# Waiting for both projection banks before the gate product of a feed-forward round

## The reference

```python
def swiglu(h, w13, w2):
    g, u = jnp.split(h @ w13, 2, axis=-1)
    return (jax.nn.silu(g) * u) @ w2
...
        x = x + swiglu(rmsnorm(x, norm_ffn_g[i]), f_w13[i], f_w2[i])
```

## Time and profile before

| | |
|---|---|
| median of 3 runs | 2007.06 us (2005.67 to 2007.57) |
| profiled execution, its own time | 2005.67 us |
| its span, first to last instruction | 2003.9 us |
| PE busy | 1915.3 us, 96% of the span |
| DVE busy | 1376.5 us, 69% |
| ACT busy | 923.3 us, 46% |
| mean granted clock of TensorE | 0.986 of full speed |

### The profile page before, as it was taken

One profiled execution on the slowest core, in us unless ns is written; L12 is line 12 of the kernel. 1 busy time (PEld: TensorE's weight loads), 2 busy tenths in 40 slices (PEclk: granted clock), 3 DMA queues, 4 the chain that ended last, 5 costly groups with the idle time before them and its releaser, 6 DMA issues.

```text
span 2003.9 us, 32582 instructions
## 1 busy us (share of the span) xinstructions
PE 1915.3 (96%) x13424; PEld 1741.9 (87%) x13424; DVE 1376.5 (69%) x1577; ACT 923.3 (46%) x990; POOL 46.3 (2%) x65
## 2 busy tenths in 40 slices
PE   6999988999999988999999999999998999999999
PEld 6998887777777778999989999996878999999998
DVE  4777975766677656766667646668997666676565
ACT  4544843655666554443345444334334333444332
POOL 0000000000000000001101000000000000000000
PEclk8999999999999999999999999999999999999999
DMA  7553352787677756555554376553313655555553
GB/s 217 183 168 99 112 160 78 283 294 268 251 286 282 289 164 181 190 184 194 189 168 135 105 215 203 196 173 126 106 64 130 206 190 188 170 188 180 194 192 105
DMA packets 243916, 366.03 MB, mean 183 GB/s; under 512 B 12566, under 2 KB 217962, under 8 KB 231402
## 3 DMA queue, kind: packets, MB, share of 16 engines
q1 hardware_dynamic: 243817, 364.64, 54.2%
HBM read 363.57 MB, written 1.05 MB: 182 GB/s over the span
## 4 chain that ended last, share of the span: by engine, by line
PE 60%; DVE 10%; DMA 6%; ACT 4%; issue 3%; SPq 1%; DVEq 0%; POOL 0%; ACTq 0%
PE proj L931 32%; PE acc L1265 10%; PE proj L950 6%; DMA raw<-in_w_exp_up_dram 6%; PE proj L1449 3%; DVE ring_lo L3111 2%; ACT ring_hi L2153 2%; ACT second_hi L2153 1%; PE acc L1419 1%; DVE ring_lo L2426 1%; PE acc L1278 1%; DVE second_lo L3111 1%; PE acc L1525 1%; DMA raw<-in_f_w_dram 1%; PE proj L1717 1%
## 5 line engine op out<-in xcount | busy, mean ns | idle before, releaser
L2426 DVE TENSOR_TENSOR ring_lo<-raw,ring_hi 128x2048 fp32r<-128x2048 f32 x242 | 560.0, 2317 | 217.0 <-ACT ring_hi L1865 215.5
L1865 ACT ACTIVATE ring_hi<-raw 128x2048 fp32r<-128x2048 f32 x242 | 462.4, 1914 | 447.7 <-PE proj L931 207.3
L931 PE MATMUL proj<-h_hi,ring_hi 128*128 128x256 f32 x1424 | 407.9, 286 | 10.5 <-DVE ring_lo L2426 10.5
L931 PE MATMUL proj<-h_lo,ring_hi 128*128 128x256 f32 x1424 | 396.1, 278 | 0.0
L931 PE MATMUL proj<-h_hi,ring_lo 128*128 128x256 f32 x1424 | 395.9, 278 | 0.0
L931 PE MATMUL proj<-g_hi,ring_hi 128*128 128x256 f32 x1088 | 303.9, 279 | 1.2 <-DVE g_lo L2470 1.2
L931 PE MATMUL proj<-g_lo,ring_hi 128*128 128x256 f32 x1088 | 302.7, 278 | 0.0
L931 PE MATMUL proj<-g_hi,ring_lo 128*128 128x256 f32 x1088 | 302.7, 278 | 0.0
L931 PEld LDWEIGHTS proj<-h_hi,ring_hi 128*128 128x128 f32 x1424 | 268.8, 189 | 22.9 <-DVE ring_lo L2426 11.3
L931 PEld LDWEIGHTS proj<-h_lo,ring_hi 128*128 128x128 f32 x1424 | 269.5, 189 | 4.1 <-issue 3.2
L931 PEld LDWEIGHTS proj<-h_hi,ring_lo 128*128 128x128 f32 x1424 | 268.8, 189 | 0.0
(11 more groups left out here) (441 smaller groups left out, 3415.2 us busy)
## 6 DMA issues: line engine op xcount, KB each, us to landing
raw<-in_f_w_dram SPq DMA_DIRECT2D x132, 1024.0 KB, 5.0
raw<-in_w_exp_gate_dram SPq DMA_DIRECT2D x32, 1024.0 KB, 4.8
raw<-in_w_exp_up_dram SPq DMA_DIRECT2D x32, 1024.0 KB, 4.9
raw<-in_w_exp_down_dram SPq DMA_DIRECT2D x32, 1024.0 KB, 4.9
raw<-in_w_in_dram SPq DMA_DIRECT2D x29, 1024.0 KB, 5.5
raw<-in_a_w_in_dram SPq DMA_DIRECT2D x24, 1024.0 KB, 5.1
raw<-in_b_w_qkv_dram SPq DMA_DIRECT2D x12, 1024.0 KB, 5.1
raw<-in_c_w_in_dram SPq DMA_DIRECT2D x12, 1024.0 KB, 5.1
```

The costliest lines, as they stand in the source:

```text
L931: last = pe.matmul(bank[:, a, :], w[:, k, a * P:(a + 1) * P], h[:, k, :], start=(k == 0 and w is hi and h is h_h and (a == 0 or not first) ...
L1865: act.activation(w_hi[n.slot][:, :], raw[n.slot][:, :], ACT.Copy).then_inc(hi_ready, 1)
L2426: dve.tensor_tensor(w_lo[n.slot][:, :], raw[n.slot][:, :], w_hi[n.slot][:, :].bitcast(f32), SUB)\
```

## The change

Ahead of gate(i+1) PE now waits for `banks_read` of round i in place of `gate_scaled` of round i, and the wait for `banks_read` ahead of up(i+1) is gone. Since DVE raises `gate_scaled` of a round before `banks_read` of the same round, the new wait covers both. PE has one wait less in each of the ten passes in each of the four nets. Nothing else differs, and no other engine's code is changed.

```diff
                 for i, c, g in mlp_rounds(pe, name):
                     wait_parts(Chunk(c, g))
-                    pe.wait_ge(gate_scaled, i + (base + 1))
+                    pe.wait_ge(banks_read, i + (base + 1))
                     product_f(Chunk(c, g), operand, False)
                     wait_parts(Chunk(c + 1, g))
-                    pe.wait_ge(banks_read, i + (base + 1))
                     product_f(Chunk(c + 1, g), operand, False)
                     wait_parts(Chunk(c + 2, g))
                     pe.wait_ge(hid_ready, i + (base + 1))
```

## The result

The changed kernel's median is 2019.17 us over 11 runs (2009.38 to 2030.27), that of the kernel before 2006.54 us over 11 runs (2004.04 to 2010.6). The ratio is 1.0057, with a 95% interval of 1.0037 to 1.0078, so some 11.4 us slower (7.4 to 15.7 us); the two medians themselves lie 12.6 us apart. The profiled execution took 2022.98 us, with a span of 2021.2 us, 17.3 us over that of before.

What follows compares the result with a forecast made beforehand. PE, busy 96% of the span, was taken as the bound. Stalls of 8.84 us, less 1.6 us of pace, plus 3.2 us of clock, made 10.4 us: 2016.8 us forecast, range 2012.5 to 2020.5 us.

Steps and rivals of the forecast that it cites:

- The place: First pass of each net, up(0) straight to gate(1): all the cost here; later passes covered by down(i-1), no existing stall removed.
- The halt: PE ahead of gate(1) waits for DVE's `hid` of round 0: 2.06 us without a matmul, gate(1) 2.22 us later.
- Halt and pace together: Per net, ahead of and in gate(1) and up(1): 2.31 us for the delayed start, less 0.41 us from faster matmuls.
- The gain of pace in gate(1) and up(1): Matmuls behind the stall go at 0.1135 instead of 0.1178 us: 0.41 us gained a net, 1.6 us in all.
- The clock: Behind two of four stalls the granted clock falls to half for 3.3 us, some 1.6 us lost each, 3.2 us.
- the five old waits: PE's waits of 1.64 to 2.16 us in the trace before the change; half clock followed three, full clock two.
- rival 1: Stall ahead of gate(1) in all four nets but clock stays full: 7.2 us slower, 2013 to 2014 us; chance 0.17.
- The term for ffn1: In ffn1 ahead of gate(2), 0.31 us of idle time and a 0.09 us slow restart vanish: 0.40 us given back.
- my rivals: Five alternatives: full clock 0.17; four slow stretches or unchanged pace 0.09; no measurable change 0.06; passes wait 0.01; faster 0.02.

Runs made afterwards that it cites:

- experiment 2: Kernel before with the new wait only in the nine later passes of each net, the first pass waiting as before: median 2009.07 us, ratio 1.0009.
- experiment 1: Kernel before with the new wait only ahead of gate(1) in each net, the nine later passes waiting as before: median 2017.31 us, ratio 1.0048.
- experiment 3: Changed kernel with DVE's first product of a net ahead of its first `ring_lo`: median 2017.99 us, ratio 1.0058 to the kernel before.
- experiments 3 and 8: experiment 3, and the changed kernel with DVE's first product of a net made twice: median 2024.81 us, ratio 1.0112 to the kernel before.

## Why the prediction came out as it did

**The place was right.** The passes cost nothing (experiment 2), the first pass has all of it (experiment 1), and no wait was taken away.

**The halt.** Forecast: 2.06 us without a matmul, `hid` to gate(1) 0.14 us, 2.22 us later than before. The trace has 2.06 and 0.14 us, and gate(1) starts 8.30 us behind `spread_inv` instead of 6.09, which is 2.21 us later. In its place in the code it is DVE's queue, and halt and net follow when that queue is cut or lengthened (experiments 3 and 8).

**Halt and pace together.** Forecast per net: 2.31 - 0.41 = 1.90 us with the clock full. ffn1 with a halt and the fast pace: 183.42 - 181.62 = 1.80 us; the filled halts cost 1.7 us. The gain of pace in gate(1) and up(1) is real but not certain: where they stay at 0.1178 us, ffn0 and ffn2 take 182.1 instead of 181.7 us.

**The clock.** Forecast per stretch: 1.6 us. 181.67 - 178.31 = 3.36 us with a fall, less the 1.80 us without, is 1.56 us. The count was mis-sized: three in four, not two, and the same three each time: 15 of 15 in ffn0, ffn2 and ffn3, 0 of 5 in ffn1. That is 1.6 us more than forecast. Taking two was not forced by the five old waits: with their 3 in 5, two and three falls in four are equally likely (0.35 each), and no fall at all has 0.03, not the 0.17 that rival 1 was given. Nor is 3 in 5 a property of the wait's length, since the same 1.64 us was followed by half clock in one trace of the kernel before and not in the other. Rival 1, and the rule of the Trainium skill behind it (TensorE: Matmul & The Clock Gate, "Why this matters for your kernels"), which warns only of longer gaps, is refuted here for three nets of four: the half clock stands in the rows behind waits of 2.04 to 2.07 us. What spares ffn1 is open; at 2.78 us it is not spared.

**The term for ffn1** (0.40 us given back) rested on one trace. The kernel before has this idle time in one of its two traces, and against the other nothing is given back. This error of 0.4 us was cancelled by another: halt and pace together cost 0.1 us less in each of the four nets than forecast.

**What was missing** is the slow pace through a whole net. I had taken 0.1178 us only as a state that ends at the first down product, with a halt ending it sooner. In the nets that holds without a halt (12 of 12) and with the halt filled (8 of 8), but behind an open halt the slow pace can stay on for the net, 187.18 - 183.42 = 3.76 us. None of my rivals had it. It could have been seen in the trace of the kernel before, outside the nets: between ffn2 and ffn3 there are 528 matmuls in a row at L931, and the two traces of that same kernel go through them at different paces, the first one first:

```profile
1729.91 0.47 PE L931 MATMUL proj<-g_hi,ring_hi 128*128 128x256 f32 x1
...
1792.28 0.28 PE L950 MATMUL proj<-ring_hi,h_hi 128*128 128x256 f32 x1
...
1728.55 0.47 PE L931 MATMUL proj<-g_hi,ring_hi 128*128 128x256 f32 x1
...
1788.59 0.28 PE L950 MATMUL proj<-ring_hi,h_hi 128*128 128x256 f32 x1
```

(1792.28 - 1729.91) / 528 = 0.1181 us, and (1788.59 - 1728.55) / 528 = 0.1137 us. So a slow pace that lasts does not need a halt of the kind that the change makes. With four nets, a trace of the changed kernel adds up to 3 x 3.4 + 1.8 = 12.0 us when none is slow and 15.8 us with ffn1 slow; against ffn1 at 181.62 us the three traces have 15.7, 12.6 and 16.2 us. The forecast of 10.4 us lies below all three but within the measured interval of 7.4 to 15.7 us, because fewer falls were counted and the slow pace was left out. That it comes within 1 us of the ratio's 11.4 us is in part luck, since that interval is 8 us wide.

**How the two hang together.** Behind none of the 19 falls of the clock was a net slow through its passes. Of the 13 open halts without a fall, 5 were. So a fall, which costs 1.6 us, may keep the net from going slow, which costs 3.3 to 4.2 us. It does not end the slow pace at once: behind three of the 19 falls gate(1) and up(1) went on at 0.1178 us at full clock, and only the first down product ended it. This is a count and not shown as a cause; what starts the pace is not settled. It would also explain why the short halt of experiment 3 wins so little: three slow nets in eight, 1.4 us a net on average, stand against the 1.6 us of the clock. The spread of the changed kernel's runs is only in part explained. A slow ffn1 makes 3.8 us of the 21 us. Outside the nets the 13 traces range from 1279.8 to 1289.8 us, and the two kernels overlap there (1280.9 and 1284.0 us before, 1284.1 to 1286.2 us changed); the stage between ffn2 and ffn3, at one pace or the other, makes 2.3 us of it.

## What to carry to other kernels

Before a wait is merged into an earlier one, look at the first pass of the loop: the work that covers it in the steady state (here a down product of 5.5 us) may not exist yet. Where PE is the bound, price a halt not by its length alone but by what PE does behind it; here 2.06 us of idle time cost 3.4 us where the clock fell, 5.6 us where the net went slow, and 1.8 us where neither happened. And where single runs differ by more than the effect, time the stage the edit touches in each trace: nets of a kind that go the same way agree within 0.6 us while runs differ by 7 to 21 us.

## What I had not expected of the hardware

A stream of 256-column matmuls has two steady paces at full clock, 0.1136 and 0.1178 us, and at the second one two forms. In the one that begins at `spread_inv`, the first down product takes 5.60 us and the passes behind it are fast; in the one that lasts, it takes 5.51 us and the passes stay slow (all 5 slow nets, against 5.60 us in the 11 nets without a halt and without a late load); the time is taken from its first matmul to the first of gate(2). Where gate(1) and up(1) are fast it takes 5.49 to 5.50 us. Which of them comes is not a matter of the code: in the two traces of experiment 3, ffn0 was fast once and slow once behind the same halt of 0.97 us.
